# Expert biases of a mixture-of-experts block: from bias matmuls on TensorE to broadcast loads and adds on VectorE

## The reference

```
gu = xb @ w_gate_up[e] + b_gate_up[e]          # 128 rows, 1024 -> 2048
gate, up = gu[:, :1024], gu[:, 1024:]
gate = minimum(gate, 7.0)
up = clip(up, -7.0, 7.0)
act = (up + 1) * (gate * sigmoid(1.702 * gate))
y = act @ w_down[e] + b_down[e]                # 1024 -> 1024
```

## Time and profile before

| | us |
|---|---|
| median of 3 runs | 1726.53 (1725.62 to 1729.35) |
| the profiled execution, whole | 1726.46 |
| its span | 1724.6 |
| TensorE busy | 1657.2 (96%) |
| VectorE busy | 1351.2 (78%) |
| ScalarE busy | 1094.6 (63%) |
| GpSimd busy | 323.4 (19%) |

### The profile page before, as it was taken

The page is one execution under the profiler, slowest core; times in us unless marked ns, Lnnn a source line. Parts: engine busy times, 40 slices in busy tenths (PEclk is TensorE's granted clock), DMA queues, the critical chain, the costliest instruction groups (busy, mean ns, idle before and its releaser), DMA issues.

```text
span 1724.6 us, 23842 instructions
## 1 busy us (share of the span) xinstructions
PE 1657.2 (96%) x7974; PEld 1352.2 (78%) x7974; DVE 1351.2 (78%) x1089; ACT 1094.6 (63%) x989; POOL 323.4 (19%) x178
## 2 busy tenths in 40 slices
PE   7999999999987979999999999999999999999995
PEld 5797777888975758888888888888888888888884
DVE  4864555633546969999999999999999999999994
ACT  5323434322343657778777787778877788777873
POOL 0000000600004742122211321122211221112210
PEclk9999999999996989999999999999999999999998
DMA  8231222332535799999999999999999999999993
GB/s 269 74 97 51 73 74 74 92 122 74 180 146 186 266 322 364 377 364 376 381 385 372 361 381 382 380 373 365 382 379 377 373 365 388 380 373 364 377 387 82
DMA packets 211683, 482.34 MB, mean 280 GB/s; under 512 B 12539, under 2 KB 55075, under 8 KB 195123
## 3 DMA queue, kind: packets, MB, share of 16 engines
q1 hardware_dynamic: 201024, 453.99, 70.1%
q0 software_dynamic: 10624, 27.87, 7.9%
HBM read 469.05 MB, written 21.67 MB: 285 GB/s over the span
## 4 chain that ended last, share of the span: by engine, by line
PE 89%; POOL 3%; DVE 2%; issue 2%; DMA 2%; ACT 1%; SPq 0%; ACTq 0%; POOLq 0%; DVEq 0%
PE ps L575 27%; PE ps L577 27%; PE ps L576 27%; PE ps L755 2%; PE ps L761 2%; PE ps L779 2%; POOL slot_records L1487 1%; PE ps L689 1%; PE ps L678 1%; DMA out<-r 1%; PE ps L650 1%; DMA r<-in_x 1%; PE ps L669 0%; POOL work L1506 0%; PE ps L722 0%
## 5 line engine op out<-in xcount | busy, mean ns | idle before, releaser
L1236 DVE TENSOR_TENSOR zT<-raw,zT 128x2048 fp32r<-128x2048 f32 x96 | 221.4, 2307 | 70.4 <-ACT zT L988 67.1
L1236 DVE TENSOR_TENSOR w_lo<-more_raw,w_hi 128x2048 fp32r<-128x2048 f32 x96 | 218.0, 2298 | 15.9 <-ACT w_hi L988 15.8
L1236 DVE TENSOR_TENSOR zT<-more_raw,zT 128x2048 fp32r<-128x2048 f32 x96 | 220.0, 2291 | 4.0 <-ACT zT L988 4.0
L1236 DVE TENSOR_TENSOR w_lo<-raw,w_hi 128x2048 fp32r<-128x2048 f32 x96 | 217.3, 2290 | 0.0
L575 PE MATMUL ps<-w_hi,xT 128*128 128x512 f32 x512 | 216.3, 422 | 0.0
L575 PE MATMUL ps<-zT,xT 128*128 128x512 f32 x512 | 204.7, 400 | 10.9 <-DVE zT L1236 10.9
L988 ACT ACTIVATE zT<-more_raw 128x2048 fp32r<-128x2048 f32 x96 | 183.4, 1911 | 33.9 <-PE ps L577 33.9
L576 PE MATMUL ps<-zT,xT 128*128 128x512 f32 x512 | 201.2, 393 | 0.0
L577 PE MATMUL ps<-zT,xT 128*128 128x512 f32 x512 | 201.1, 393 | 0.0
L577 PE MATMUL ps<-w_hi,xT 128*128 128x512 f32 x512 | 201.0, 393 | 0.0
L576 PE MATMUL ps<-w_lo,xT 128*128 128x512 f32 x512 | 200.9, 392 | 0.0
(11 more groups left out here) (244 smaller groups left out, 3358.7 us busy)
## 6 DMA issues: line engine op xcount, KB each, us to landing
more_raw<-in_w_gate_up SPq DMA_DIRECT2D x129, 1024.0 KB, 6.0
raw<-in_w_gate_up SPq DMA_DIRECT2D x127, 1024.0 KB
raw<-in_w_down SPq DMA_DIRECT2D x65, 1024.0 KB
more_raw<-in_w_down SPq DMA_DIRECT2D x63, 1024.0 KB, 6.7
raw<-in_w_in SPq DMA_DIRECT2D x29, 1024.0 KB, 5.2
r<-in_x SPq DMA_DIRECT2D x8, 512.0 KB, 7.1
raw<-in_w_branch_conv SPq DMA_DIRECT2D x4, 1024.0 KB, 4.7
raw<-in_w_out SPq DMA_DIRECT2D x4, 1024.0 KB, 4.7
```

The source lines that it names most:

```text
L1236: nc.vector.tensor_tensor(expert_pair(1, c), chunk, expert_pair(0, c).bitcast(F32), ALU.subtract).then_inc(split_lo, 2)
```

## The change

The gate and up biases no longer go through TensorE. SyncE loads the expert's bias row, broadcast over 128 partitions, for each block and half (two loads of 512 KB in SBUF for each block). VectorE adds them when a half is finished: `add_bias` writes gate + bias to `g1b` and up + bias to `u1b`, in place of `clamp_up`. ScalarE's `sigmoid` now waits for `gate_biased`, and has four instructions in place of two: Relu and Sigmoid for the gate, and two Relus that clip up. `activate` reads the gate from SBUF; `activate(g, 1)` moves behind chunk 11. The bias matmuls, `bpart`, `sel` and the GpSimd work on them are gone.

The first block is put in another order: chunk 3 is split ahead of the placing of records, the gates are turned after j = 9 instead of j = 3, the down biases are multiplied after j = 13 and after the first rows are turned, and are added in pairs of banks. GpSimd writes x2 to `out` before it gathers and before `over_experts`, which is shorter.

```diff
+            def load_bias(e, half):
+                row = b_gate_up[0][bass.ds(e, 1)].rearrange("o (s h n) -> h o s n", s=2, h=2)[half]
+                sp.dma_start(bias[:, half], row.to_broadcast([P, 2, 512])).then_inc(bias_in[half], 16)
+            def next_bias(g, c, e):
+                if c in (4, 8):
+                    half = c // 4 - 1
+                    sp.wait_ge(act_ok, 2 * g + half)
+                    load_bias(e, half)
...
                 for c in range(CPE):
+                    next_bias(g, c, g)
                     load_expert(g, c, g if c < 8 else g - 1)
...
-                if k == 0:
-                    for s in range(2):
-                        pe.matmul(ps[:, base + s, :], sel[:, bass.ds(g, 1), :],
-                                  bpart[:, D * s + 512 * half:D * s + 512 * half + 512],
-                                  start=True, stop=False)
...
-                if j == 3:
+                if j == 9:
                     pe.wait_ge(gates_ok, 1)
...
-                if j == 7:
+                if j == 13:
                     pe.wait_ge(gT_ok, 1)
                     pe.wait_ge(down_bias_in, 16 * NB)
+                    pe.wait_ge(act_ok, 2)
                     down_bias(0)
-                if j == 11:
-                    pe.wait_ge(x2_biased, 1)
-                    down_bias(1)
-            pe.wait_ge(x2_biased, 2)
             next_rows(0, 0)
             next_rows(0, 1)
+            pe.wait_ge(x2_biased, 2)
+            down_bias(1)
+            pe.wait_ge(x2_biased, 4)
...
             def sigmoid(g, half):
-                sc.wait_ge(used, unit_base(g) + (8 * half + 8))
-                nc.scalar.activation(g1b, ps[:, bk_A + 2 * half, :], ACT.Relu, scale=-1.0,
-                                     bias=stat[:, 24:25]).then_inc(gate_clamped, 1)
-                sc.wait_ge(gate_clamped, 2 * g + half + 1)
-                sc.wait_ge(act_ok, 2 * g + half + 1)
-                nc.scalar.activation(sgb, g1b, ACT.Sigmoid, scale=-ALPHA,
+                n = 2 * g + (half + 1)
+                sc.wait_ge(gate_biased, n)
+                nc.scalar.activation(sgb, g1b, ACT.Relu, scale=-1.0, bias=stat[:, 24:25]).then_inc(gate_clamped, 1)
+                sc.wait_ge(gate_clamped, n)
+                nc.scalar.activation(sgb, sgb, ACT.Sigmoid, scale=-ALPHA,
                                      bias=stat[:, 25:26]).then_inc(sigmoid_ok, 1)
+                sc.wait_ge(up_biased, n)
+                nc.scalar.activation(u1b, u1b, ACT.Relu, scale=-1.0, bias=stat[:, 24:25]).then_inc(up_low, 1)
+                sc.wait_ge(up_low, n)
+                nc.scalar.activation(u1b, u1b, ACT.Relu, scale=-1.0, bias=stat[:, 26:27]).then_inc(up_clamped, 1)
...
             with sc.Fori(1, nblk) as g:
+                sc.wait_ge(x2_biased, 4)
                 store_y(g, unit_base(g), g)
...
             split_expert(0, 2)
+            split_expert(0, 3)
             place_records()
...
-            def clamp_up(g, half):
+            def add_bias(g, half):
                 ve.wait_ge(used, unit_base(g) + (8 * half + 8))
                 ve.wait_ge(act_ok, 2 * g + (half + 1))
-                nc.vector.tensor_scalar(u1b, ps[:, bk_A + 2 * half + 1, :], LIMIT, -LIMIT, ALU.min,
-                                        ALU.max).then_inc(up_clamped, 1)
+                ve.wait_ge(bias_in[half], 16 * g + 16)
+                nc.vector.tensor_tensor(g1b, ps[:, bk_A + 2 * half, :], bias[:, half, 0, :],
+                                        ALU.add).then_inc(gate_biased, 1)
+                nc.vector.tensor_tensor(u1b, ps[:, bk_A + 2 * half + 1, :], bias[:, half, 1, :],
+                                        ALU.add).then_inc(up_biased, 1)
...
-                nc.vector.scalar_tensor_tensor(sgb, ps[:, bk_A + 2 * half, :], LIMIT, sgb, ALU.min,
-                                               ALU.mult).then_inc(gate_up_ok, 1)
+                nc.vector.scalar_tensor_tensor(sgb, g1b, LIMIT, sgb, ALU.min, ALU.mult).then_inc(gate_up_ok, 1)
...
-                nc.vector.scalar_tensor_tensor(act[:, half, :], u1b, 1.0, sgb, ALU.add,
+                nc.vector.scalar_tensor_tensor(act[:, half, :], u1b, 1.0 - LIMIT, sgb, ALU.add,
                                                ALU.mult).then_inc(act_ok, 1)
...
+                for pair, bank in ((slice(0, 2), bk_A), (slice(2, 4), bk_D)):
+                    nc.vector.tensor_tensor(x2[:, pair, cols], x2[:, pair, cols], ps[:, bank:bank + 2, :],
+                                            ALU.add).then_inc(x2_biased, 1)
...
                     if c == 6:
-                        clamp_up(g, 0)
+                        add_bias(g, 0)
                     if c == 7:
                         activate(g, 0)
                     if c == 10:
-                        clamp_up(g, 1)
+                        add_bias(g, 1)
                         turned(g, ROWS0, xTh[:, 0:4, :], xTl[:, 0:4, :], bk_T)
+                    if c == 11:
                         activate(g, 1)
...
+            gp.wait_ge(x2_biased, 4)
+            for b in range(NB):
+                gp.dma_start(out_v[:, b, :], x2[:, b, :]).then_inc(out_set, 16)
+            gp.dma_start(out[S:S + P, :], x2[:, 0, :]).then_inc(out_set, 16)
             gp.wait_ge(slots_in, 16)
             gather_next(1)
             over_experts()
-            gp.wait_ge(x2_biased, 2)
-            for b in range(NB):
-                gp.dma_start(out_v[:, b, :], x2[:, b, :]).then_inc(out_set, 16)
-            gp.dma_start(out[S:S + P, :], x2[:, 0, :]).then_inc(out_set, 16)
-            over_selectors()
```

More of the change, by code:

```diff
@@ L287, in hybrid_block @@
         tb23 = r3[:, HPG * NSH * P:].rearrange("p (h g n) -> p h g n", h=HPG, g=2)
[L288 to L292, removed]
+        bias = r3[:, 0:2 * D].rearrange("p (h s n) -> p h s n", h=2, s=2)
+        lgT = r3[0:NE, 2 * D:2 * D + S]
         cu = work[:, 0:1024].rearrange("p (m s) -> p m s", m=2)
@@ L361, in hybrid_block @@
             sem(n) for n in ("down_bias_in", "gates_ok", "gT_pe", "gT_ok", "down_bias_pe", "x2_biased")]
-        bias_in, bias_parts_ok = sem("bias_in"), sem("bias_parts_ok")
+        bias_in = [sem(f"bias_in{half}") for half in range(2)]
         xs_set, ix_set = sem("xs_set"), sem("ix_set")
@@ L371, in hybrid_block @@
         xs_in = sem("xs_in")
-        gate_clamped, up_clamped, gate_up_ok, sigmoid_ok = [sem(n) for n in ("gate_clamped", "up_clamped", "gate_up_ok", "sigmoid_ok")]
+        gate_biased, up_biased, gate_clamped, up_low, up_clamped, gate_up_ok, sigmoid_ok = [sem(n) for n in (
+            "gate_biased", "up_biased", "gate_clamped", "up_low", "up_clamped", "gate_up_ok", "sigmoid_ok")]
         act_ok = sem("act_ok")
@@ L499, in _ @@
                     sp.wait_ge(logits_ok, PAIRS)
-                    for part in range(3):
-                        sp.dma_start(braw[NE * part:NE * part + NE, :], b_gate_up[0]).then_inc(bias_in, 16)
+                    load_bias(0, 0)
+                    load_bias(0, 1)
                 if CHUNKS[c] == ("wo", 3):
@@ L558, in _ @@
                     for c in range(CPE):
+                        next_bias(g, c, e)
                         load_expert(g, c, e if c < 8 else before)
@@ L808, in down_bias @@
                 for b in range(NB):
-                    last = pe.matmul(ps[:, bk_D + b, :], gT[NE * b:NE * b + NE, :],
+                    last = pe.matmul(ps[:, bk_A + 4 * (b // 2) + b % 2, :], gT[NE * b:NE * b + NE, :],
                                      bdn[NE * b:NE * b + NE, 512 * n:512 * n + 512], start=True, stop=True)
@@ L1000, in _ @@
             sc.wait_ge(logitsT_pe, 1)
-            sc.wait_ge(bias_parts_ok, 1)
+            sc.wait_ge(logits_ok, PAIRS)
             nc.scalar.activation(lgT, ps[0:NE, 0, :], ACT.Copy).then_inc(logitsT_ok, 1)
@@ L1089, in _ @@
             nc.vector.memset(stat[:, 25:26], ALPHA * LIMIT)
+            nc.vector.memset(stat[:, 26:27], 2 * LIMIT)
             nc.vector.memset(stat[:, 31:32], EPS).then_inc(eps_ok, 1)
@@ L1394, in add_down_bias @@
                 cols = slice(512 * n, 512 * n + 512)
-                nc.vector.tensor_tensor(x2[:, :, cols], x2[:, :, cols], ps[:, bk_D:bk_D + NB, :],
-                                        ALU.add).then_inc(x2_biased, 1)
-            for c in range(3, 8):
+                for pair, bank in ((slice(0, 2), bk_A), (slice(2, 4), bk_D)):
+                    nc.vector.tensor_tensor(x2[:, pair, cols], x2[:, pair, cols], ps[:, bank:bank + 2, :],
+                                            ALU.add).then_inc(x2_biased, 1)
+            for c in range(4, 8):
                 split_expert(0, c)
-                if c == 3:
+                if c == 4:
                     gates_by_expert()
-                if c == 4:
+                if c == 6:
                     ve.wait_ge(gT_pe, 1)
                     nc.vector.tensor_copy(gT, ps[:, bk_D, 0:P]).then_inc(gT_ok, 1)
-                if c == 6:
-                    add_down_bias(0)
-                if c == 7:
```

(9 more changed lines are left out.)

34 lines of the change are left out of this document (6 added, 28 removed).

## The result

The changed kernel takes 1989.0 us (1987.6 to 1989.8), the kernel before 1726.4: a ratio of 1.152 (1.150 to 1.154). The forecast was 1970 us, in a range of 1925 to 2038.

The account below looks back on a forecast made before the run. The prediction took TensorE to bound the kernel before, at 35.59 us a turn. Span 1724.6, first block +1.0, thirty turns +233.6 and last turn +8.6 gave 1967.8; with 1.86 outside the span, 1970 us, range 1925 to 2038.

Parts of the forecast that it names:

- The mechanism: In each loop half, ScalarE's sigmoid waits for VectorE's add; its lead goes and the engines take turns, 9.8 us idle.
- The round: One loop turn walked through from half 0's add on VectorE and ScalarE: 34.1 us work plus 9.8 idle on VectorE.
- the fourth rival: TensorE's clock stays at 1.2 GHz from chunk 7 to 11: a turn of 50 us, 2160 us; chance 4%.
- The turn: One turn of the expert loop: 43.9 us after against 35.59 before, +233.6 us over thirty turns.
- the clock: TensorE's lower clock behind gaps before chunks 7 and 11: 1.6 us a gap, absorbed, leaving a turn at 43.8.
- The first block: Before the loop: a 4.0 us gate wait gained against a 2.7 us ScalarE chain: +1 us, bounds -4 and +8.
- The last turn: From the last turning of activations to the output copies: 32.6 us before, 41.2 after, +8.6.
- DMA: Two more 512 KB bias loads a turn: free, 14.4 MB in 43.9 us being 327 GB/s, under 374.
- The rival's price: Bias loads in the loop not hidden: 14.4 MB at 375 GB/s, 38.3 us a turn, 1793 us; chance 2%.
- the first rival: ScalarE's lead in the loop survives and VectorE is the bound: 36.8 us a turn, 1748 us; chance 4%.
- GpSimd beside VectorE: GpSimd could slow the activation's first steps, both inputs in SBUF, 0.1 us each, 6 us over 30 turns; none counted.
- The stall: In the first long turn ScalarE's output copy waits 14.3 us for GpSimd; forecast gone, all 30 turns counted alike.

Follow-up runs that it names:

- gaps_filled: The changed kernel with 12 matmuls, whose results are unused, added on TensorE ahead of chunk 7 and 9 ahead of chunk 11: 1978.9 us, ratio 1.147.
- lead_back: The changed kernel, but ScalarE's gate Relu reads PSUM without waiting for the add, and the two Relus for up are dropped: 1756.4 us, ratio 1.018.
- later_sigmoid: The changed kernel with gate Relu and Sigmoid behind chunks 7 and 11, up Relus behind chunks 8 and 0, VectorE's activations one chunk later: 1759.2 us, ratio 1.020.
- later_sigmoid_one_bias: As later_sigmoid, but bias rows are loaded once, for expert 0, and used for all blocks: 1708.7 us, ratio 0.990 to the kernel before.
- order_only: The kernel before, bias matmuls kept, with the changed kernel's first block, down biases and GpSimd order: 1716.0 us, ratio 0.994.

## Why the prediction was right, and where it was off

**The mechanism** held as it was written out. The round put VectorE's idle time at 4.2 and 2.9 us behind the adds, 1.2 before chunk 11, and, at full clock, 1.1 before chunk 3 and 0.4 before chunk 4. `gaps_filled`, which is at full clock, has 4.20, 2.81, 1.18, 1.08 and 0.34. The changed kernel has 4.20, 2.81, 1.18, then 1.24 before chunk 2 (forecast for the lower clock: 1.3), nothing before chunk 3, and 0.34 before chunk 4. `lead_back` and `later_sigmoid` show that the wait and what stands behind it make this idle time, and not the work. The clock did not stay low from chunk 7 to 11, as the fourth rival had it: it was 1.00 again from 1142.00 to 1148.40 us.

**The turn** was sized at 43.9 and is 44.33 (+0.43, or 12.9 us over 30 turns: the larger part of the 19 us by which the forecast was low). The failed step is the clock. I wrote that the lower clock puts the down steps' end back by 1.6 us, which the idle at chunk 3 absorbs, "and the turn is again 43.8". `gaps_filled` takes the clock away and gets 44.06, so 0.27 of the 0.43 is the clock after all. It lies between VectorE's chunk 0 and its chunk 4 (the first of the two that the second line holds), 11.91 us in the changed kernel and 11.61 in `gaps_filled`:

```profile
1108.28 2.28 DVE L1246 TENSOR_TENSOR w_lo<-more_raw,w_hi 128x2048 fp32r<-128x2048 f32 x1
...
1120.19 4.50 DVE L1246 TENSOR_TENSOR w_lo<-more_raw,w_hi 128x2048 fp32r<-128x2048 f32 x2 [0.34 <-ACT w_hi L993]
```
```profile
1017.26 2.28 DVE L1256 TENSOR_TENSOR w_lo<-more_raw,w_hi 128x2048 fp32r<-128x2048 f32 x1
...
1028.87 4.49 DVE L1256 TENSOR_TENSOR w_lo<-more_raw,w_hi 128x2048 fp32r<-128x2048 f32 x2 [0.34 <-ACT w_hi L1003]
```

The lower clock traded 1.08 us before chunk 3 for 1.24 before chunk 2, but the 0.34 before chunk 4, which I had let vanish too, stayed. Chunk 4 on ScalarE stands behind the second activation tile, and TensorE turns the two tiles behind its chunks 0 and 1. The slow stretch reached into its chunk 0 (first two matmuls 0.59 us apart, 0.33 in `gaps_filled`), so the first tile was turned 5.50 us behind the start of VectorE's chunk 0 instead of 5.20, and the second as much later. The other 0.16 us are small spacings: the four ScalarE instructions took 2.76 us (1127.53 to 1130.29) where I had 2.7, twice in a turn. What is left of it I can't assign.

**The first block** was +1.0 and is +5.2 us (turning of the activations at 582.58 against 577.42). The step that failed is the balance of the 4.0 us wait against one ScalarE chain: TensorE waits 7.26 us for the second pair of down-bias sums before it may start turn 1, against 2.29 us before, and a table load of 1.28 us falls into the first chain (the kernel before has it too, behind its ScalarE's lead). VectorE's work on half 1 still began 1.6 us earlier than before (570.72 against 572.30); what I had wrong is what stands between it and turn 1. The bound of +8 held it.

```profile
577.61 0.79 PE L586 MATMUL ps<-w_hi,xT 128*128 128x512 f32 x1 [7.26 <-DVE r L1409]
```

**The last turn** was +8.6 and is +9.5 (73.2 us from its turning to the end, 63.7 before). The three differences, 12.9, 4.2 and 0.9, make up the 18 us between the forecast span of 1967.8 and 1985.7. All three are too low, so none hides another.

**DMA** in the forecast: "free" at 43.9 us was right. The rival's price, 38.3 us a turn, was too high: the rate rose to 389 GB/s and the turn is 37.1. I had read the rate of the kernel before as a limit, when it was what that kernel needed.

**VectorE as the bound:** 36.8 us a turn for the first rival was too high as well. It added the idle time and gaps of the kernel before to the new work; `later_sigmoid_one_bias` runs at 35.29 with the same work. That idle was slack, not need.

**GpSimd beside VectorE** was counted at nothing, and in the changed kernel nothing shows: the first step of the activation takes 0.685 us in the median, where it took 0.681.

**The stall** was counted right, as gone in the changed kernel: its turns from 582.58 on are all 44.1 to 44.4. But it did not say which edit removes it, and it had the selector work end before the loop. `order_only` still has the stall in its trace. In the changed kernel there are no selectors, the arithmetic that is left is shorter and ends at 597.3 us, inside turn 1, and ScalarE's next output copies begin at 623.07 us, well after it.

## What to carry to other kernels

In these runs two engines that feed each other, each in the order of its program, were busy nearly all the time only while one led. Before an edit makes the leader wait for the follower, look in the timelines for how far it leads (3.2 us here) and for what stands in its program behind the new wait; in these runs the follower paid for it nearly microsecond by microsecond (two Relus, 1.4 us, were 1.4 us of its wait for chunk 7). If the dependency can't be avoided, put it behind the next piece of work that the follower needs: that alone took 230 of 263 us away.

## What I had not expected of the hardware

A DMA share of 1.03 did not say that the rate had reached its end: it stood at 1.03 with 376 GB/s and with 389. The lower clock came behind gaps of 2.29 and 2.42 us on TensorE. Behind the 2.42 us gap the first matmuls still ran at 0.23 us apart, and the lower clock came within the same chunk. The same mean clock, 0.92, went with turns of 44.07 and of 44.37 us: what counted was where in the turn the slow stretch lay. Filling gaps with needless matmuls gained 9 to 10 us. One chunk of VectorE took 5.03 us instead of 2.29 beside a long compare on GpSimd, while the chunk before it, beside the same compare, took 2.28.
